# A delta rule on unnormalised keys, and one block-diagonal 128x128 matrix a head in its scan

## What is computed

```python
q, k, v = silu(centred_depthwise_conv(concat([q, k, v]), conv_w))      # split in three
q = l2_normalize(q) * (GDN_HD ** -0.5)
k = l2_normalize(k)
# for each direction, chunks of 64 tokens, gc the running sum of the log decay g:
decay = exp(where(i >= j, gc_i - gc_j, -inf))
lower = where(i > j, (k * beta) @ k.T * decay, 0.0)
sol = triangular_solve(lower + eye, concat([v * beta, k * beta * exp(gc)]))
u, w = sol[..., :128], sol[..., 128:]
# scan over the chunks
v_new = u - w @ state
out = (q * exp(gc)) @ state + ((q @ k.T) * decay) @ v_new
state = state * exp(g_last) + (k * exp(g_last - gc)).T @ v_new
# both directions
o = o_f + o_b
o = o * rsqrt(mean(o * o) + EPS) * norm_g * silu(z)
```

## Time and profile before

| | |
|---|---|
| median of 3 runs | 1715.95 us (1715.75 to 1716.82) |
| the profiled execution | 1716.34 us |
| its span | 1714.5 us |
| TensorE busy | 1683.5 us |
| VectorE busy | 1160.8 us |
| ScalarE busy | 950.8 us |
| mean granted TensorE clock | 0.998 |

### The profile page before, as it was taken

The page is one execution under the profiler, slowest core; times in us unless marked ns, Lnnn a source line. Parts: engine busy times, 40 slices in busy tenths (PEclk is TensorE's granted clock), DMA queues, the critical chain, the costliest instruction groups (busy, mean ns, idle before and its releaser), DMA issues.

```text
span 1714.5 us, 24757 instructions
## 1 busy us (share of the span) xinstructions
PE 1683.5 (98%) x10226; PEld 1386.5 (81%) x10226; DVE 1160.8 (68%) x1833; ACT 950.8 (55%) x1476; POOL 10.1 (1%) x22
## 2 busy tenths in 40 slices
PE   8999999999999999999999999999999999999998
PEld 6777888877778887888888888888888888878886
DVE  6976885679688667555686577655575556885554
ACT  7734644477155446444576767544564456974443
POOL 0000000000000000000000000000000000000000
PEclk9999999999999999999999999999999999999999
DMA  6322445542234555555544334655555555454553
GB/s 261 123 77 99 166 156 195 184 169 100 81 139 149 192 189 184 196 176 193 212 171 170 123 117 178 222 188 196 200 205 175 195 208 197 147 176 181 196 174 146
DMA packets 41872, 291.70 MB, mean 170 GB/s; under 512 B 4672, under 2 KB 4928, under 8 KB 7712
## 3 DMA queue, kind: packets, MB, share of 16 engines
q1 hardware_dynamic: 39312, 280.68, 45.6%
q0 software_dynamic: 2304, 8.91, 1.5%
q10 hardware_dynamic: 144, 0.52, 0.1%
HBM read 289.05 MB, written 1.05 MB: 169 GB/s over the span
## 4 chain that ended last, share of the span: by engine, by line
PE 81%; DVE 13%; ACT 3%; issue 2%; DMA 1%; SPq 0%; DVEq 0%; ACTq 0%
PE pg L477 24%; PE pg L479 24%; PE pg L478 24%; DVE wl L1985 3%; PE ps L846 2%; PE ps L665 2%; DMA raw<-weights 1%; ACT wh L1338 1%; PE ps L889 1%; PE ps L649 0%; PE ps L948 0%; PE ps L1233 0%; DVE hTl L2556 0%; PE ps L1188 0%; PE ps L1118 0%
## 5 line engine op out<-in xcount | busy, mean ns | idle before, releaser
L477 PE MATMUL pg<-wh,hTh 128*128 128x512 f32 x2092 | 833.2, 398 | 2.4 <-DVE hTl L2556 0.9
L479 PE MATMUL pg<-wh,hTl 128*128 128x512 f32 x2092 | 816.5, 390 | 0.0
L478 PE MATMUL pg<-wl,hTh 128*128 128x512 f32 x2092 | 815.4, 390 | 0.0
L1985 DVE TENSOR_TENSOR wl<-raw,wh 128x1024 fp32r<-128x1024 f32 x512 | 602.6, 1221 | 192.0 <-ACT wh L1338 188.7
L1338 ACT ACTIVATE wh<-raw 128x1024 fp32r<-128x1024 f32 x522 | 522.8, 1054 | 204.5 <-DMA raw<-weights 194.2
L477 PEld LDWEIGHTS pg<-wh,hTh 128*128 128x128 f32 x2092 | 393.2, 188 | 86.5 <-issue 8.3
L479 PEld LDWEIGHTS pg<-wh,hTl 128*128 128x128 f32 x2092 | 392.8, 188 | 84.0
L478 PEld LDWEIGHTS pg<-wl,hTh 128*128 128x128 f32 x2092 | 393.5, 188 | 75.1
L1444 ACT ACTIVATE arena<-pg,sm 128x256 f32<-128x256 f32 (+1 forms) x67 | 36.6, 546 | 239.9 <-PE pg L479 239.8
L2643 DVE SCALAR_TENSOR_TENSOR arena<-pg,sm,arena 128x256 f32<-128x256 f32 x88 | 38.5, 479 | 156.0 <-ACT arena L1445 156.0
L1404 ACT ACTIVATE hTh<-ps 128x512 fp32r<-128x512 f32 x60 | 33.6, 597 | 31.0 <-PE ps L665 31.0
(11 more groups left out here) (391 smaller groups left out, 1148.7 us busy)
## 6 DMA issues: line engine op xcount, KB each, us to landing
raw<-weights SPq DMA_DIRECT2D x265, 1024.0 KB, 4.8
arena<-wide POOLq DMA_DIRECT2D x9, 512.0 KB, 3.6
raw<-weights SPq DMA_DIRECT2D x2, 512.0 KB, 5.9
cst<-const_tables POOLq DMA_DIRECT2D x1, 1024.0 KB, 5.2
plainh<-dist_tables POOLq DMA_DIRECT2D x2, 512.0 KB, 5.7
arena<-gate_mix POOLq DMA_DIRECT2D x1, 1024.0 KB, 5.8
x<-x_in ACTq DMA_DIRECT2D x1, 512.0 KB, 4.0
x<-x_in SPq DMA_DIRECT2D x1, 512.0 KB, 9.2
```

The source lines that it names most:

```text
L477: pe.matmul(dst, lh, rh, start=first, stop=False)
L478: pe.matmul(dst, lh, rl, start=False, stop=False)
L479: return pe.matmul(dst, ll, rh, start=False, stop=last)
L1985: tt(wl[:, slot, h], raw[:, slot, h], wh[:, slot, h], ALU.subtract)\
```

## The change

- q and k are no longer normalised. The matrices behind the silu (`cvp`, which now are `qnT` and `knT` themselves) are used as they are; `normalized` and `features` go, with 16 transposes of 128x128 a layer. Each transposed-back k is copied once to `kn` by ScalarE (`kn_ready`). The norms of q and k are taken together (`norms`) and enter as factors: beta times k's norm scales the values (`VS`: half of them on VectorE in place of a copy, half on ScalarE in the inversion), beta times the norm squared stands in `BETAJ` and `NEGS`, q's norm enters in `delta_result`.
- The rows of the decays go to banks 0 and 1 of the convolution, before the waits for `back_read` and `v_read`; the Gram products go to banks 2 and 3 behind them.
- The scores and the solution of a scan step are written into one matrix of 128x128 a head, with the directions' 64x64 blocks on its diagonal (`diagonal`, `T_DIAG`, `SC_DIAG`); GpSimd zeroes the other blocks (`zeros_ready`). L897 and L915 become one matmul with 128 rows a head. The scaling by beta behind the inversion goes; its last additions write into the diagonal blocks, half a direction by ScalarE.
- Of the retention's masks ScalarE makes the first half during the inversion, VectorE adds the second (`both_ways`) there, and ScalarE takes the exponential behind the scan.
- The two visits of a chunk are summed once behind the scan (`o_sum`), not in each step. Units are split in halves at fixed places of the scan. `small_turned` comes one chunk of the second gemm later, and the cumulated rows one prepared chunk after `second_back`.

```diff
+        def diagonal(t):
+
+            cols = 512 * (t % 2)
+            return (heads(v) for v in (T_DIAG[t // 2][:, cols:cols + 512], SC_DIAG[:, 512 * t:512 * t + 512]))
...
-        SC_, LMASK = xn[:, 0:1024], xn[:, 1024:2048]
+        SC_, LMASK, SC_DIAG = XT_, TM_, xn
...
-        squares, qn = V(11264, 2048), V(13312)
+        cvp = [qnT, knT, V(10240)]
+        squares = V(12288, 2048)
...
+        T_DIAG = (TB, spare(plainl, 8))
...
-                gemm(D, (512,), ("evac_act",), inside={(0, 2): first_turn, (0, 3): small_turned(16), (1, 3): first_back})
-                gemm(D, (512,), ("evac_act",), inside={(0, 1): second_turn, (1, 0): first_features, (1, 1): cumulated,
-                                                       (1, 3): back_and_rows})
-                prepare(2)
+                gemm(D, (512,), ("evac_act",), inside={(0, 2): first_turn, (1, 0): small_turned(16), (1, 3): first_back})
+                gemm(D, (512,), ("evac_act",), inside={(0, 1): second_turn, (1, 1): cumulated, (1, 3): second_back})
+                prepare(1)
+                cumulated_rows()
+                prepare(1)
                 c.wait("cum_t_read")
                 pe.wait_ge(sem["evac_act"], st.evacs["evac_act"])
                 turn(2)
-                prepare(3)
-                c.wait("qk_ready")
-                features(kn, 2)
-                prepare(3)
-                c.wait("feat_read")
+                prepare(6)
+                c.wait("sq_ready")
+                c.wait("kn_ready")
...
                 last.then_inc(sem["row_done"], 1)
+                c.wait("back_read")
+                c.wait("v_read")
...
                 c.wait("inv_scaled")
-                TB4, SC4, S3 = blocks(TB), blocks(SC_), heads(STATE, 8)
+                c.wait("vs_ready", 4)
+                c.wait("inv_copied")
+                c.wait("zeros_ready")
...
-                        for d, m, r in places[t]:
-                            rhs = RV[half(r), h * P:(h + 1) * P] if t else VS[half(r), 0, h * P:(h + 1) * P]
-                            last = pe.matmul(ps[half(r), 0, h * P:(h + 1) * P], TB4[half(r), 4 * d + h, m, :], rhs,
-                                             start=True, stop=True)
+                        rhs = RV[:, h * P:(h + 1) * P] if t else VS[:, 0, h * P:(h + 1) * P]
+                        last = pe.matmul(ps[:, 0, h * P:(h + 1) * P], t_diag[:, h, :], rhs, start=True, stop=True)
...
-                            last = pe.matmul(ps[half(r), 1, h * P:(h + 1) * P], SC4[half(r), 4 * d + h, m, :],
-                                             VN[half(r), h * P:(h + 1) * P], start=True, stop=True)
+                        last = pe.matmul(ps[:, 1, h * P:(h + 1) * P], sc_diag[:, h, :], VN[:, h * P:(h + 1) * P],
+                                         start=True, stop=True)
...
-                features(qnT, 0)
                 convolved(1)
                 square(1)
+                for m in range(M):
+                    last = act.activation(kn[:, 512 * m:512 * m + 512], ps[:, 2 + m, :], ACT.Copy)
+                last.then_inc(sem["kn_ready"], 1)
...
-                c.wait("mask_arg")
-                act.activation(MASKS, MASKS, ACT.Exp).then_inc(sem["mask_ready"], 1)
+                    act.activation(LT[:, 512 * d:512 * d + 512], ps[:, d, :], ACT.Copy).then_inc(sem["low_t_read"], 1)
                 prepare(4)
                 act.activation(DELTA_Z, DELTA_Z, ACT.Silu).then_inc(sem["delta_z_ready"], 1)
+                c.wait("norms_ready")
                 for level in range(5):
                     prepare(1)
+                    if level < 4:
+                        t, d = ((0, 0), (1, 0), (2, 1), (3, 1))[level]
+                        m, r = scan_chunk(t, d)
+                        for h in range(NH):
+                            v, o = VS[half(r), t, h * P:(h + 1) * P], 8 * m + 4 * d + h
+                            last = act.activation(v, v, ACT.Copy, scale=BETA_NK[half(r), o:o + 1])
+                        last.then_inc(sem["vs_ready"], 1)
+                        if level == 0:
+                            act.wait_ge(sem["dist_landed"], 16 * (l + 1))
+                        act.activation(MASKS[:, 512 * level:512 * level + 512],
+                                       DIST.rearrange("p (s n) -> p s n", s=2)[:, 0, :], ACT.Copy,
+                                       scale=LAM[:, level:level + 1]).then_inc(sem["mask_first"], 1)
                     prepare(1)
+                c.wait("inv_yt", 5)
+                new = ps[:, 1, 0:256].rearrange("p (h m f) -> p m h f", m=M, f=CHUNK)
+                for m in range(M):
+                    for r in range(2):
+                        dst, _ = diagonal(2 * m + r)
+                        last = act.activation(dst[half(r), 2:4, half(r)], new[half(r), m], ACT.Copy)
+                last.then_inc(sem["inv_copied"], 1)
...
+                c.wait("o_sum")
                 act.activation(Lm, o_acc, ACT.Square).then_inc(sem["sq_done"], 1)
+                c.wait("mask_arg")
...
+                def square_sums(t):
 
                     c.wait("sq_ready")
-                    c.step(dve.tensor_reduce(STATS, squares[:, 1024 * t:1024 * t + 1024].rearrange("p (k e) -> p k e", e=HD),
-                                             AX.X, ALU.add))
-                    rstd_of(STATS, 1.0)
-                    if t == 0:
-                        c.step(ts(STATS, STATS, HD ** -0.5, None, ALU.mult))
-                    src = ps[:, 2 * t:2 * t + 2, :].rearrange("p m (h e) -> p (m h) e", h=NH)
-                    c.sig(tt(heads(dst, 8), src, over(STATS, HD), ALU.mult), "qk_ready")
-
-                normalized(0, qn)
+                    return dve.tensor_reduce((NQ, NK)[t], squares[:, 1024 * t:1024 * t + 1024]
+                                             .rearrange("p (k e) -> p k e", e=HD), AX.X, ALU.add)
+
+                def norms():
+
+                    c.step(square_sums(1))
+                    prepare(4)
+                    rstd_of(NORMS, 1.0)
+                    c.step(ts(NQ, NQ, HD ** -0.5, None, ALU.mult))
+                    tt(NQ2, NQ, NQ, ALU.mult)
+                    k_norms = NK.rearrange("p (m h) -> p m h", m=M).unsqueeze(1).broadcast_to([P, 2, M, NH])
+                    c.step(tt(by_direction(BETA_NK), by_direction(BETA), k_norms, ALU.mult))
+                    c.sig(tt(by_direction(BETA_NK2), by_direction(BETA_NK), k_norms, ALU.mult), "norms_ready")
+                    c.step(dve.tensor_copy(BETAJ.rearrange("p (j m) -> p j m", m=M),
+                                           BETA_NK2.rearrange("p (m j) -> p j m", m=M)))
...
-                normalized(1, kn)
+                square_sums(0)
                 gemm(D, (512,), ("evac_act",), ahead=2)
                 ret_qk_read[0] = st.evacs["evac_act"] + 3
                 later_taps(2)
-                prepare(7)
+                norms()
                 c.wait("back_tr", 3)
                 for t, d in ((0, 1), (1, 1), (2, 0), (3, 0)):
                     m, r = scan_chunk(t, d)
-                    last = dve.tensor_copy(VS[half(r), t, :], ps[half(r), 2 + m, :])
+                    o = 8 * m + 4 * d
+                    last = tt(heads(VS[half(r), t, :]), heads(ps[half(r), 2 + m, :]), over(BETA_NK[half(r), o:o + 4], P),
...
+                c.wait("row_done")
+                tt(X3, ps[:, 0:2, :].rearrange("p b (q f) -> p (b q) f", f=CHUNK), over(GCJ, CHUNK),
+                   ALU.subtract).then_inc(sem["dist_ready"], 1)
                 for d, js in enumerate(both):
-                    tt(LM3[:, js, :], times(MASK["los" if d == 0 else "ups"], 8), over(BETAJ[:, js], CHUNK), ALU.mult)
-
-                c.wait("row_done")
-                tt(X3, ps[:, 2:4, :].rearrange("p b (q f) -> p (b q) f", f=CHUNK), over(GCJ, CHUNK),
-                   ALU.subtract).then_inc(sem["dist_ready"], 1)
-                retention_masks(l)
+                    last = tt(LM3[:, js, :], times(MASK["los" if d == 0 else "ups"], 8), over(BETAJ[:, js], CHUNK),
+                              ALU.mult)
+                c.step(last)
+                prepare(6)
+                dve.wait_ge(sem["dist_landed"], 16 * (l + 1))
                 c.wait("decay_ready")
...
+                SC6 = SC_DIAG.rearrange("p (m r h e) -> p m r h e", m=M, r=2, h=NH)
+                for r in range(2):
+                    tt(SC6[half(r), :, r, :, half(r)], SC5[half(r), 0], QK4[half(r)], ALU.mult)
+                    for m in range(M):
+                        last = tt(SC6[half(r), 1 - m, 1 - r, :, half(r)], SC5[half(r), 1, m], QK4[half(r), m], ALU.mult)
                 c.step(last)
+                prepare(4)
...
+                    if s == 2:
+                        c.wait("cum_exp")
+                        for t in range(1, 4):
+                            for d in range(2):
+                                m, r = scan_chunk(t, d)
+                                o = 8 * m + 4 * d
```

(56 more changed lines are left out.)

101 lines of the change are left out of this document (35 added, 66 removed).

## The result

| | before | after |
|---|---|---|
| median, runs alternating on one chip | 1716.52 us (1715.75 to 1716.97) | 1700.72 us (1700.37 to 1701.54) |
| ratio, 95% interval | | 0.9908 [0.9897, 0.9918] |
| span of the profiled run | 1714.5 us | 1698.8 us |

The kernel is 15.8 us faster. The first part of the page answers to the earlier trace rows: TensorE's busy time fell by 9.5 us and its idle time by 6.2 (from 31.0 to 24.8).

A forecast was written before the change was run, and what follows sets the result against it. TensorE, busy for 98% of the span, was taken as the bound, with VectorE's timeline deciding. Layer sums of -4.7 and -3.7 made -8.4 us, 1716.34 to 1707.9 (1707.6 beside the median); range 1703.5 to 1713.5.

The forecast's parts named there:

- part 4: Scan: matmuls give nothing, within -0.1 to +0.1 us for each of 16 groups; vanishing waits give -1.6 us a layer.
- Rival (d): TensorE's "issue" waits at level 16, 1.3 and 1.6 us, go or shrink: 1705 us; chance 12%.
- own case: The forecast's main account for the whole kernel: 1705 to 1711 us, chance 51%.
- Start of the chain: Before the inversion: VectorE's taps of v start 5.0 us earlier in layer 0, 4.0 in layer 1.
- Rival (c): TensorE's clock halves in the inversion after a new stall, costing 1.6 us each time: 1709.5 to 1711 us; chance 15%.
- part 2: VectorE's chain from the taps of v to `inv_x`, 28.8 us before, grows by 1.3 us a layer.
- In the inversion: At level 8 VectorE has no idle time, so 0.7 us more work makes TensorE wait: +0.4 us a layer.
- The scan's waits: In the scan, waits for the first `VD` (0.6 us with restart) and for an output (0.55 us) go.
- Tail: Behind the scan, two small products of 0.2 us each stand before `y_ready`: +0.2 us a layer.
- Rival (b): VectorE's scattered 64-partition products cost double, or GpSimd's memsets hold VectorE up: 1714 us; chance 13%.
- (a): Full-array matmuls in the scan's diagonal groups cost twice a pair of tiles: +17.6 us, 1725 us; chance 4%.
- (e): The gain is given back, later stages being held by VectorE or weights at fixed times: 1716 us; chance 5%.

The follow-up runs named there:

- the kernel with the copies moved: Changed kernel with VectorE's copies into the doubled matrices moved from ahead of level 8 to ahead of level 16: 1700.70 us, ratio 0.9906.
- pairs: Changed kernel with the diagonal products of t_diag and sc_diag formed again as two 64x64 matmuls a head: 1703.68 us, ratio 0.9921.

## Why the prediction fell short

1. *The failed step is part 4: "The matmuls themselves give nothing", with its bounds of -0.1 and +0.1 us for each of 16 groups.* It compared busy times, 1.1 and 1.1 us, which hide what lies at a group's borders. Measured: -0.32 for each of 16 groups, 5.1 of the 7.4 us that were missed. The trace of before said so: in the earlier trace rows eight full transposes at 47.17 are followed by the chunk at 48.01, 0.84 us later, while 16 of L897 take 1.02 to their chunk. The Trainium skill names a mechanism in the very page that was weighed (TensorEngine Tiling (Array Packing), Key Properties): changing the tiling mode, not just the tile, drains the TensorE. The trace agrees that such a change costs time, and gives the price; that the time is a drain, no run here shows. The rule that was weighed instead, that tiles give up to 2x (Theoretical Speedup on that page of the Trainium skill), holds in its direction where steps are saved (state products: 1.10 us as tiles, 1.70 over the full array). There is nothing to save where the block-diagonal matrix takes as many steps as the pair.
2. *Rival (d), the "issue" stall, came true in layer 0* (1.28 us of idle time; the group at level 16 takes 2.94 us instead of 4.44) and partly in layer 1 (1.57 became 1.14, at another level). It had 12% and stood outside the own case. It was right that the stall hangs on what stands before it; that it could also come back was not in it.
3. *Start of the chain*: -5.5 in layer 0 against -5.0, and -4.8 in layer 1 against -4.0. The small turn was sized rightly: 1.1 us, counted at 1.0. The miss lies on TensorE's way to `second_back`, which comes 2.5 and 1.85 us earlier where 2.05 and 1.1 were foretold; what gave the rest there is open. Behind it ScalarE's chain is 3.0 shorter in both layers, as foretold, although the terms listed for it add up to 59.4 us and not to 59.05. Length 30.35 against 30.1. So the inversion starts 3.95 and 3.30 earlier, not 3.7 and 2.7.
4. *Rival (c), the clock, came true too, and cost nothing*, in the way that it named. TensorE's windows, layer 0 and then layer 1 after, and layer 1 of the kernel with the copies moved, where TensorE came to the same place and kept its clock:

```profile
74.00:75.00 1.00, 1.00 (x25) 0.50 0.00 0
...
391.00:392.00 1.00, 1.00 (x24) 0.50 0.00 0
```

```profile
391.00:392.00 1.00, 1.00 (x42) 1.00 0.00 0
```

   At 0.50, 1.2 GHz, behind the row products and the stall of 1.3 us, the Gram products take 3.26 us instead of 2.02. Where the clock holds, TensorE waits for `inv_x` instead: 1.24 us in the kernel with the copies moved, 0.17 after, and the inversion starts at 407.48 in both. VectorE's chain sets the time, as part 2 had it.
5. *In the inversion* the wait behind level 8 is 0.31, and 0.39 from start to start, foretold 0.4; moving the copy took it away. *The scan's waits* gave 1.1 us (pairs against before), foretold 1.1 to 1.2, and L2274's 0.4 went.
6. *Tail*: +0.5 and +0.75 against +0.2. TensorE reaches the result earlier than VectorE and waits 0.8 (L2388); with pairs, when it comes later, 0.26. A part of the scan's gain is given back there, some 0.5 us a layer.
7. *Rival (b) fell*: the scattered score products take 0.68 and 0.37 us, the usual rate. GpSimd's sixteen memsets of 64x256 lie at 23.86 to 29.33 us in layer 0; VectorE's chain behind started no later than foretold. Beside them VectorE split a unit (L1997 at 24.99) in 2.36 us, as it did before (L1985 at 24.84), so they took nothing from it. Rivals (a) and (e) fell too: a full group costs less than a pair group, not twice, and 15.7 of the 15.8 us stay in the span.

```profile
23.86 0.65 POOL L2989 MEMSET arena<- 64x256 f32 x2 [4.92 <-DVE sm L2115]
```

## What to carry to other kernels

Price a group of matmuls by the distance from its start to the next group's start, with the distance ahead of it, never by its busy time; then ask whether its tile form differs from its neighbours'. A short group of 64-row or 64-column tiles between full-array matmuls is worth rewriting as full ones when that takes no more steps, even if half of the array multiplies zeros. And when a total moves by a microsecond or two more than the stretch that was edited, look for stalls that moved elsewhere before giving the difference to the edit: here the tail's wait, the clock and the "issue" stall each did.
